# Two chained transformer blocks on one core: start-up loads, their waits and the room of the stick weights rearranged

## The reference, cut to what matters

```python
# first block, layer 0: window attention with a sink, over x and ctx
h = rms_norm(x, norm_g) * (1 + scale) + shift           # front of every stage
q, k, v, g = split(h @ a_w_in, [1024, 1280, 1536]); q, k = rope(q), rope(k)
p = softmax(concat([q @ k.T * scale, sink]))[..., :-1]  # sink: one number per head, 16 heads
x = x + gate * ((p @ v * silu(g)) @ a_w_out)
# first block, layer 1: latent attention
cq, ckv, kr, g = split(h @ b_w_in, ...); q = rms_norm(cq, q_norm) @ w_uq; kv = rms_norm(ckv, kv_norm) @ w_ukv
x = x + gate * ((softmax(q @ k.T) @ v * silu(g)) @ b_w_out)
x = rms_norm(x, final_g)
# second block, layer 0: half the width retention, half "stick breaking" attention
z = rmsnorm(h, norm_gain) @ even_w_in                    # [1024, 4096]: q k v g of retention, q k v g of stick
o_a = retention(q_a, k_a, v_a); o_b = stick_breaking(q_b, k_b, v_b)
h = h + concat([o_a * silu(g_a), o_b * silu(g_b)]) @ even_w_out; h = h + sigmoid(h @ ple_gate) * (p @ ple_proj)
# second block, layer 1: rwkv7, then the same gate, then the last norm
xs = hn + (token_shift(hn) - hn) * mu                    # six mixed streams
r, k, v, g = xs[:4] @ odd_w_in; decay, a = low-rank products of xs[4], xs[5]; scan over tokens; @ odd_w_out
```

## Time and profile before

| | us |
|---|---|
| median of 3 runs | 4628.16 (4627.15 to 4633.45) |
| the profiled execution's own time | 4627.72 |
| its span, first to last instruction | 4625.9 |
| PE busy | 4178.1 (90% of the span) |
| DVE, ACT, POOL busy | 1576.8, 1360.7, 318.9 |

### The profile page before, as it was taken

The page is one execution under the profiler, slowest core; times in us unless marked ns, Lnnn a source line. Parts: engine busy times, 40 slices in busy tenths (PEclk is TensorE's granted clock), DMA queues, the critical chain, the costliest instruction groups (busy, mean ns, idle before and its releaser), DMA issues. The chain is left out here.

```text
span 4625.9 us, 70564 instructions
## 1 busy us (share of the span) xinstructions
PE 4178.1 (90%) x29426; PEld 2466.5 (53%) x29426; DVE 1576.8 (34%) x2944; ACT 1360.7 (29%) x2322; POOL 318.9 (7%) x143
## 2 busy tenths in 40 slices
PE   7997989979989999898897998897999978888798
PEld 1445864435556666544454446443444457888443
DVE  0335651213235444321332017112222246666111
ACT  0116752212245555421121228211222222221132
POOL 0000000000000000000000000000000025665000
PEclk9998999989999999999998999998999989999899
DMA  7100020031241111000201000203211121111300
GB/s 266 60 1 4 2 83 0 0 76 43 78 133 32 31 31 32 16 0 5 87 0 73 0 0 1 91 0 126 83 50 50 45 96 58 62 49 44 137 14 23
DMA packets 154507, 229.26 MB, mean 50 GB/s; under 512 B 81623, under 2 KB 92055, under 8 KB 153241
## 3 DMA queue, kind: packets, MB, share of 16 engines
q1 hardware_dynamic: 154270, 225.78, 14.6%
HBM read 175.21 MB, written 50.54 MB: 49 GB/s over the span
## 5 line engine op out<-in xcount | busy, mean ns | idle before, releaser
L221 PE MATMUL psum<-rp_w,rp_mixed 128*128 128x512 f32 x1024 | 445.4, 593 | 6.5 <-DVE rp_mixed L2150 3.0
L221 PEld LDWEIGHTS psum<-rp_w,rp_mixed 128*128 128x128 f32 x1024 | 193.2, 190 | 246.5 <-issue 240.3
L1345 PE MATMUL psum<-la_kT,la_qT 96*128 96x512 f32 (+1 forms) x768 | 299.3, 526 | 14.8 <-DMA la_v<-latent_v 12.5
L2278 POOL TENSOR_TENSOR rs_kk<-rs_k,rs_k_k 128x1024 f32<-128x1024 f32 x7 | 16.5, 2361 | 3883.7 <-DVE rs_k L2622 3764.3
L1287 DVE TENSOR_SCALAR_CACHE_REDUCE la_s<-psum 128x1280 f32<-128x1280 f32 x128 | 190.9, 1491 | 236.7 <-PE psum L1345 236.7
L221 PE MATMUL psum<-sp_w,sp_hT 128*128 128x512 f32 x512 | 223.5, 597 | 27.8 <-DMA sp_w<-in_even_w_in_dram 19.0
L221 PE MATMUL psum<-output_wo,pg_oT 128*128 128x512 f32 x512 | 230.9, 610 | 12.0 <-DMA output_wo<-in_even_w_out_dram 5.9
L221 PE MATMUL psum<-output_wg,pg_xT 128*128 128x512 f32 x512 | 227.5, 603 | 7.3 <-ACT pg_xT L1910 7.3
L221 PE MATMUL psum<-retention_w,ret_hT 128*128 128x512 f32 x512 | 223.6, 598 | 5.8 <-DMA retention_w<-in_even_w_in_dram 5.8
L1275 ACT ACTIVATE la_pT<-psum 128x512 f32<-128x512 f32 x256 | 139.0, 595 | 288.4 <-PE psum L1363 288.4
L1345 PEld LDWEIGHTS psum<-la_kT,la_qT 96*128 96x128 f32 x768 | 136.6, 191 | 140.2 <-issue 127.2
(11 more groups left out here) (409 smaller groups left out, 7079.8 us busy)
## 6 DMA issues: line engine op xcount, KB each, us to landing
ada_slots<-in_ada_w_dram SPq DMA_DIRECT2D x12, 2048.0 KB, 19.3
rwkv_raw<-x_rows SPq DMA_DIRECT2D x48, 512.0 KB, 2.6
rp_w<-in_odd_w_in_dram SPq DMA_DIRECT2D x4, 4096.0 KB, 29.7
retention_w<-in_even_w_in_dram SPq DMA_DIRECT2D x4, 2048.0 KB, 18.3
sp_w<-in_even_w_in_dram SPq DMA_DIRECT2D x1, 8192.0 KB
output_wg<-in_ple_gate_dram SPq DMA_DIRECT2D x2, 4096.0 KB, 23.2
latent_v<-lp_v SPq DMA_DIRECT2D x10, 512.0 KB, 2.6
la_kT<-latent_kT SPq DMA_DIRECT2D x16, 320.0 KB, 4.5
```

Source lines behind the costliest of these rows:

```text
L221: last = pe.matmul(out[:, c:c + w], left[:, k, :], right[:, k, c:c + w], start=(k == 0), stop=(k == kd - 1))
L1345: last = pe.matmul(s_banks[:, c:c + n], qT[:, s, q * P:(q + 1) * P], kT[:, s, c:c + n], start=True, stop=True)
L2278: eng.tensor_tensor(kk[:, :], k[s][:, :], k_k[:, :], ALU.mult).then_inc(q["kk_made"], 1)
```

## The change

Nine stages are touched (the window and latent calls of `gate_and_project` share one function).

1. Waits on small loads stand in front of the first instruction that reads them: the rope table in `window_qkv`, the latent gain in `latent_projections`, the norm's columns in `stick_projections`, and `mu` (with a semaphore of its own) in `rwkv_projections`.
2. The sink comes in one DMA of 16 numbers to each partition; DVE brings it into pairs with two copies, and scales it with two instructions.
3. `w_q` and the gate weights `wg` come in two DMAs of 512 columns each, with a wait for each half. In `window_qkv` they come ahead of the table.
4. In `retention`, `w0` comes ahead of the tables. SP then waits until the last tile's q and k are projected and loads the stick's `w0` and `w1` into the room of retention's; it waits until the last tile's v and g are projected and loads `w2` and `w3`. `stick_projections` uses them there, and has no weights of its own. `stick_breaking` has `soft` and `row` in the room of `w0` and `w1`.

```diff
@@ class Weights
-        self.at = {n: ...sbuf_tensor(...) for n, (shape, _) in sources.items()}
+        self.at = {n: ...sbuf_tensor(...) for n, (shape, _) in sources.items()} if room is None else room
@@ window_qkv
+                w = weight_blocks(a["a_w_in"][0])
+                for half in range(2):
+                    cols = slice(half * BANK, (half + 1) * BANK)
+                    sp.dma_start(w_q[:, :, cols], w[:, :, cols]).then_inc(q_in[half], 16)
                 sp.dma_start(table[:, :, :, :], a["rope_a"].rearrange("t p c d -> p t c d")).then_inc(table_in, 16)
-                w = weight_blocks(a["a_w_in"][0])
-                sp.dma_start(w_q, w[:, :, 0:D]).then_inc(q_in, 16)
                 sp.dma_start(w_kv[:, :, :], w[:, :, D:D + 2 * KV]).then_inc(kv_in, 16)
...
-                dve.wait_ge(table_in, 16)
                 scaled(0)
                 columns(0)
                 scaled(1)
                 for i in range(NT):
                     if i + 1 < NT:
                         columns(i + 1)
+                    if i == 0:
+                        dve.wait_ge(table_in, 16)
                     rope_half(i, 0)
...
-                    if i == 0:
-                        pe.wait_ge(q_in, 16)
                     for half in range(2):
+                        pe.wait_ge(q_in[half], 16) if i == 0 else None
@@ window_attend
-                for g in range(2):
-                    for b in range(2):
...
-                        sp.dma_start(dst, src.partition_broadcast(P), allow_slow_non_contiguous=True).then_inc(sink_in, 16)
+                sp.dma_start(sink_rows[:, :], a["a_sink"][0].partition_broadcast(P)).then_inc(sink_in, 16)
...
-                dve.tensor_scalar(sink_scaled[:, :], sink[:, :], 1.0 / SCALE, None, ALU.mult).then_inc(sink_made, 1)
+                for g in range(2):
+                    dve.tensor_copy(paired(sink, g), by_head(g)).then_inc(sink_made, 1)
+                    dve.tensor_scalar(paired(sink_scaled, g), by_head(g), 1.0 / SCALE, None, ALU.mult).then_inc(sink_made, 1)
@@ gate_and_project
-                    product(pe, g_banks, front.hT[:, :, :], wg[:, :, :], g_made)
+                    if i == 0:
+                        pe.wait_ge(weights.arrived["wg0"], 16)
+                    product(pe, g_banks[:, 0:BANK], front.hT[:, :, :], wg0[:, :, :])
+                    if i == 0:
+                        pe.wait_ge(weights.arrived["wg1"], 16)
+                    product(pe, g_banks[:, BANK:], front.hT[:, :, :], wg1[:, :, :], g_made)
@@ latent_projections
-                dve.wait_ge(gain_in, 32)
                 scaled(0)
                 columns(0)
                 scaled(1)
-                dve.wait_ge(table_in, 16)
                 for s in range(STEPS + 1):
                     if s + 1 < STEPS:
                         columns(s + 1)
+                    if s == 0:
+                        dve.wait_ge(gain_in, 32)
+                        dve.wait_ge(table_in, 16)
@@ retention, SP
                 sp.dma_start(norm_columns[:, :], ...).then_inc(norm_in, 16)
+                weights.load(sp, ("w0",))
...
-                weights.load(sp)
+                weights.load(sp, ("w1", "w2", "w3"))
+                sp.wait_ge(qk_made, X_TILES)
+                next_weights.load(sp, ("w0", "w1"))
+                sp.wait_ge(z_made, X_TILES)
+                next_weights.load(sp, ("w2", "w3"))
@@ stick_projections
-                sp.dma_start(w[:, :, :], weight_blocks(a["even_w_in_2"][0])[:, :, 4 * W:]).then_inc(w_in, 16)
...
-                dve.wait_ge(norm_in, 16)
                 front.dve_scale(dve, 0, x(0))
+                dve.wait_ge(norm_in, 16)
                 front.dve_columns(dve, 0)
...
-                pe.wait_ge(w_in, 16)
+                for n in range(4):
+                    pe.wait_ge(weights.arrived[f"w{n}"], 16)
...
-                    product(pe, core.banks(2, 4), front.hT[:, :, :], w[:, :, :], z_made)
+                    for n in range(3):
+                        product(pe, core.banks(2 + n), front.hT[:, :, :], w[n][:, :, :])
+                    product(pe, core.banks(5), front.hT[:, :, :], w[3][:, :, :], z_made)
@@ stick_breaking
-        soft, row, wT = sb("soft", [P, 2, N]), sb("row", [P, ROWS, N]), sb("wT", [P, 2, BANK])
+        soft, row = (t[:, :, :].rearrange("p k n -> p (k n)").rearrange("p (u n) -> p u n", n=N) for t in room)
+        wT = sb("wT", [P, 2, BANK])
@@ rwkv_projections
-                dve.wait_ge(small_in, (1 + STREAMS) * 16)
...
                 front.dve_scale(dve, 0, x(0))
+                dve.wait_ge(small_in, 16)
                 front.dve_columns(dve, 0)
                 difference(0)
+                dve.wait_ge(mu_in, STREAMS * 16)
                 mix(0, 0)
```

More of the change, by code:

```diff
@@ L730, in gate_and_project @@
         sb = lambda n, shape: mem.enter_context(nc.sbuf_tensor(f"{name}_{n}", shape, F32))
[L731 removed]
+        wg0, wg1, wo = (weights.at[n] for n in ("wg0", "wg1", "wo"))
         silu, og, ogT, gate = sb("silu", [P, D]), sb("og", [P, D]), sb("ogT", [P, KD, P]), sb("gate", [P, 2, D])
@@ L1400, in _, with retention @@
                 passes(pe, run)
-def retention(nc, core, a, weights, o):
+def retention(nc, core, a, weights, next_weights, o):
     name = "ret"
@@ L1609, in _, with stick_projections @@
                 attend(X_TILES - 1, False)
-def stick_projections(nc, core, a, o, qT, kT, v):
+def stick_projections(nc, core, a, weights, o, qT, kT, v):
     name = "sp"
@@ L2857, in program @@
         both = ((ctx_tiles, True), (x_tiles, False))
-        w_gate = ([P, KD, D], weight_blocks(a["a_w_in"][0][:, D + 2 * A_KV * A_DIM:]))
+        halves = lambda name, w: {f"{name}{n}": ([P, KD, BANK], weight_blocks(w)[:, :, n * BANK:(n + 1) * BANK]) for n in range(2)}
         with ExitStack() as layer:
@@ L2869, in program @@
             with ExitStack() as held:
-                weights = Weights(nc, held, "window_gate", {"wg": w_gate, "wo": ([P, KD, D], weight_blocks(a["a_w_out"][0]))})
+                weights = Weights(nc, held, "window_gate", {**halves("wg", a["a_w_in"][0][:, D + 2 * A_KV * A_DIM:]), "wo": ([P, KD, D], weight_blocks(a["a_w_out"][0]))})
                 with stage(nc):
@@ L2895, in program @@
                     f"w{n}": ([P, KD, width], even_w[:, :, n * width:(n + 1) * width]) for n in range(4)})
+                stick_weights = Weights(nc, held, "stick", {
+                    f"w{n}": ([P, KD, width], even_w[:, :, (4 + n) * width:(5 + n) * width]) for n in range(4)}, room=weights.at)
                 with stage(nc):
-                    retention(nc, core, a, weights, o)
+                    retention(nc, core, a, weights, stick_weights, o)
+                with ExitStack() as heads:
+                    qT, kT = (heads.enter_context(nc.sbuf_tensor(n, [P, R_HEADS, X_TILES * P], F32)) for n in ("stick_qT", "stick_kT"))
+                    v = heads.enter_context(nc.sbuf_tensor("stick_v", [P, X_TILES, R_HEADS * R_DIM], F32))
+                    with stage(nc):
+                        stick_projections(nc, core, a, stick_weights, o, qT, kT, v)
+                    with stage(nc):
+                        stick_breaking(nc, core, a, o, qT, kT, v, [weights.at[f"w{n}"] for n in range(2)])
             output_weights = lambda mem, layer, w_out: Weights(nc, mem, f"output{layer}", {
-                "wo0": ([P, KD, BANK], weight_blocks(w_out)[:, :, 0:BANK]), "wo1": ([P, KD, BANK], weight_blocks(w_out)[:, :, BANK:]), "wg": ([P, KD, D], weight_blocks(a["ple_gate_2"][layer])),
+                **halves("wo", w_out), "wg": ([P, KD, D], weight_blocks(a["ple_gate_2"][layer])),
                 "wp": ([P, 2, D], weight_blocks(a["ple_proj_2"][layer]))})
-            with ExitStack() as heads:
-                qT, kT = (heads.enter_context(nc.sbuf_tensor(n, [P, R_HEADS, X_TILES * P], F32)) for n in ("stick_qT", "stick_kT"))
-                v = heads.enter_context(nc.sbuf_tensor("stick_v", [P, X_TILES, R_HEADS * R_DIM], F32))
-                with stage(nc):
-                    stick_projections(nc, core, a, o, qT, kT, v)
-                with stage(nc):
-                    stick_breaking(nc, core, a, o, qT, kT, v)
             with ExitStack() as held:
```

40 lines of the change are left out of this document (20 added, 20 removed).

## The result

The changed kernel takes **4577.63 us** (median of 4 runs, 4568.07 to 4584.03) against 4629.68 for the kernel before (4 runs, 4627.15 to 4633.45): a ratio of 0.9881, 95% interval 0.9864 to 0.9898. The forecast was 4571.5 with a range of 4561 to 4586. Run again beside other runs of before, it took 4570.82 (0.9874, 0.9858 to 0.9891). The profiled execution took 4582.14 us, 45.6 less than the profiled one of before, where the sum had 56.6.

The account below looks back on a forecast made before the run. PE, busy 90% of the span, was taken as the bound, so earlier stage starts move stage ends. 6.7 + 18.3 + 6.5 + 6.0 + 3.1 + 17.8 - 1.8 = 56.6 us, giving 4571.5 us, range 4561 to 4586.

Parts of the forecast that it names:

- window_qkv: First product of window_qkv: PE starts at 122.3 when hT is ready, the first half of w_q already there; 6.7 us gained.
- the mask's 18.3: Start of window_attend: the mask, issued 0.4 us after the sink, lands at 362.4 instead of 380.7; 18.3 us gained.
- gate_and_project: Window's gate_and_project: PE starts on the first half of wg instead of the whole; 6.5 us gained, latent call 0.
- latent_projections: Start of latent_projections: scaling no longer waits for the gain's columns, weights w come last at 1014.7; 6.0 us gained.
- retention: Start of retention: w0 ahead of the tables starts PE 4.5 us earlier, a 1.4 us wait for w1 leaves 3.1.
- stick_projections: Start of stick_projections: all four weight blocks land under the previous stage, PE starts when hT is ready; 17.8 us gained.
- rwkv_projections: K's product in rwkv_projections: its weights' landing fixes its start, a longer pause before it lowers the clock; 1.8 us lost.
- The rest: All stages without a term of their own, such as rwkv_scan and latent_attention with its gate: 0 us.
- its own range: Whole time, 4562 to 4580, chance 0.80: mask bounds, retention, the rwkv loss, and 5.4 us either way for lower-clock stretches.
- the halves land together: Rival in window_qkv and gate_and_project: two DMAs in one queue share it; 11.2 us less gain, 4582.7; chance 0.08.
- the stick's loads are not hidden: Rival in stick_projections: the barrier holds the loads back; 4589.3 without the 17.8, or 4576.3 with two blocks held; chance 0.05.
- 55.4: Sum of gains in us if loads are priced by the skill's DMA rule, 4.8 us per 2 MB more, instead of rows.

Follow-up runs that it names:

- a3: The kernel before with the sink's part alone, one contiguous 64-byte broadcast to each partition in place of four of 4-byte pieces: 4614.29 us, ratio 0.9967.
- a4: The kernel before with the stick's weights alone, loaded into retention's room under its last tile: 4611.24 us, ratio 0.9954.
- b3: The changed kernel with the stick's four loads issued in stick_projections itself, behind the barrier: 4596.34 us, ratio 0.9919.
- c1: The kernel of b1 with G's weights issued behind the first tile's first store: rwkv_projections 538.4 us, single whole time 4570.36 us.
- c2: The changed kernel with G's weights issued behind the first tile's first store: rwkv_projections 540.9 us, single whole time 4578.59 us.
- b4: The changed kernel with mu in one DMA, retention's w1 ahead of its tables, and the window's sink and mask and stick's mask loaded a stage earlier: 4566.39 us.
- b2: The changed kernel with the first products of window_qkv and the window's gate_and_project waiting for both weight halves: 4585.32 us, ratio 0.9900.
- c3: The changed kernel with G's weights behind the first store and mu loaded as 48 rows and turned by PE: rwkv_projections 534.4 us, single whole time 4570.72 us.
- b1: The changed kernel with its rwkv_projections part undone, so DVE waits for mu ahead of its first scaling again: 4576.41 us.

## Why the prediction was right, step by step

The kernel is bound by PE, and each stage's start moved its end, nearly as the sum supposed: 57.2 us gained up to rwkv_scan, 56.6 forecast. That the two agree so closely is luck in part. Single terms were off by up to 2.6 us and cancelled: more than forecast came from rwkv_projections (2.6), stick_projections (1.7) and retention (1.3), less from the two window stages (1.7), from latent_attention with its gate (1.8), and from the window's gate_and_project and latent_projections (0.5 and 0.6).

- **window_qkv** (6.7): PE starts 7.1 us behind the first statistics' start at 115.29. It gained what was said. With the mask's 18.3, measured 18.2, the two stages should give 25.0; they gave 22.5 and 24.2 in the two profiles. The sum moved each start and left what follows at its old length. In the first profile the first 16 records of PE's product took 10.21 us instead of 9.06, with more of them at the lower clock (9.03 in the second), and the 32 maxima of window_attend spread over 31.8 us (31.3 in the second, 31.4 in a3) instead of 30.9. These make 2.0 of the 2.5 us that are missing in the first profile, and 0.4 of 0.8 in the second; the rest is open.
- **gate_and_project** (6.5): 5.7 and 6.2. PE still waits for the first half, 3.58 us. **latent_projections** (6.0): 5.4 in the mean, bound by `w`, as said; the first product there took 13.9 us instead of 12.6, a part of which the stage made up.
- **retention** (3.1): the new wait for `w1` is 1.72 us where 1.4 was forecast; the stage gained 4.4 in the mean.
- **stick_projections** (17.8): 17.9 in a4 over its three stages, and 19.5 in the mean here; b3 shows that the cover of the last tile is all of it. (Before, the stage took 284.5 and 287.2 us in two profiles, so the last microsecond of this is scatter.) The loads were across the barrier in time: the second pair was issued at 2460.8, its first landed 8.8 us later, and PE needed both at 2480.9, with no wait for either.
- **rwkv_projections** (-1.8): the step that failed. "So no gain; and a loss": the slow product came, 2.8 us longer in place of 1.8, but the end of K's product does not set the end of the stage. With the old waits V's product is held by the first store, which stands behind 16 MB of weights. The loss went into that wait of 2.06 us, which I had not listed, and the stage came out 0.8 us shorter in the mean. c1 and c2 show both halves of this. The low-rank products came 3.2 us sooner in the stage, not 7.2: their next wait was for the low-rank weights. And the pause of 1.37 us that the step was read from was the shortest of four.
- **The rest** (0): rwkv_scan took 6.2 us more in the mean of two profiles, and its scatter of 20 us over all runs is more than all the terms' errors. latent_attention with its gate took 1.8 more; a3, which does not touch it, has 882.1 too, and b4 has 879.7 as before, so this is not shown to be the change's. The forecast allowed 5.4 us either way for stretches of lower clock and named no stage that scatters by itself. The two medians, 4577.63 and 4570.82, lie inside its own range of 4562 to 4580, but two of the first four times do not (4582.14 and 4584.03), and that the first median did is in part luck. The bounds of that range, added up, are 4561.4 and 4579.6.

Of the rivals, that the halves land together fell with b2, and that the stick's loads are not hidden with the profile and a4. For a pair in one queue the row is 9.0 and 13.9 us from issue to landing, in a window of the trace after at 2447 us, when SP issued the stick's first pair 0.4 us apart:
```profile
DMA to landing us min/median/max: 9.0/11.5/13.9
```
So 2 MB more took 5.3 us there, the second half of `wg` cost the stage 6.1 in b2, and 6.5 was used. The mask of 320 KB landed 3.3 us behind its issue, as the rows had it. The Trainium skill, "DMA: Bandwidth & Descriptors", section "Anatomy of one DMA", would give an estimate of 4.8. The measured 5.3 and 6.1 lie between 4.8 and 6.5. By that estimate, with 1.5 for the table, the first half of `w_q` too would have come last, at 122.7, and the forecast's sum by it would be 55.0 and not 55.4. The Trainium skill, same page, section "Queues, rings and completion order", says that completion is not first-in-first-out for one issuing engine; no pair here whose two landings are in the trace shows the later one landing first or both at once.

## What to carry to other kernels

Price a load that bounds a start by its rows, and then ask for each start what comes next: here it was the columns of `hT` in three stages (in one of them with a wait for the second block behind it), and another load in three. A loss or gain inside a stage counts only if no later wait takes it up, so follow the chain a few products on; here a store behind 16 MB of weights in the same queue swallowed it. Take a pause that a step rests on from more than one profile: this one was 1.37 us in one and 2.29 to 3.17 in three others. And before judging a few microseconds by the whole time, cut the traces by stage: one stage that nobody touched scattered by 20 us.

## What the runs showed of the hardware

- Four broadcasts of four 4-byte pieces to each of 128 partitions held the first maximum until 21.9 us behind the first issue; with one broadcast of 64 contiguous bytes it comes at 3.8. The 2048 pieces passed at some 108 a microsecond with a DMA share of 0.05; `mu`'s 6144 pieces of the same size, without a broadcast, had a share of 0.59 and were down within 8 us of the first issue.
- 6144 pieces of 4 bytes take 4.2 us of SP's time for issuing, as six DMAs (4.16 us for the six, before) or as one (0.58 us, and 4.17 for the next issue, b4); as 48 rows of 512 bytes they do not, and the next issue takes 0.42 us (c3).
- After a pause of 3.57 us K's product took 16.76 us at a granted clock of 0.83 (after), after 2.84 us 13.97 at 1.00 and after 2.65 us 16.76 at 0.83 (K's and V's products, b1); after 3.17 us K's product took 13.97 (a3): the length of the last pause alone does not decide whether the granted clock falls.
